# A one-core decoder layer on Trainium2: the running sum of w_down is kept in the output tensor in DRAM instead of in SBUF for ten of eleven groups

## The reference

```python
x = _layernorm(DN_ALPHA * x + mix @ w_out[l], ln1_g[l], ln1_b[l])
gate, up = jnp.split(x @ w_gate_up[l], 2, axis=-1)
x = _layernorm(DN_ALPHA * x + (jax.nn.silu(gate) * up) @ w_down[l], ln2_g[l], ln2_b[l])
```

## Time and profile before

| | |
|---|---|
| median of 3 runs | 2036.58 us (2036.22 to 2038.27) |
| profiled execution, its own time | 2035.88 us |
| profiled execution, span | 2034.1 us |
| PE busy | 2016.6 us, 99% |
| DVE busy | 1310.5 us, 64% |
| ACT busy | 677.4 us, 33% |
| POOL busy | 361.4 us, 18% |
| DMA traffic | 214.06 MB, mean 105 GB/s |
| granted TensorE clock, mean | 0.997 |

### The profile page before, as it was taken

The page is one execution under the profiler, slowest core; times in us unless marked ns, Lnnn a source line. Parts: engine busy times, 40 slices in busy tenths (PEclk is TensorE's granted clock), DMA queues, the critical chain, the costliest instruction groups (busy, mean ns, idle before and its releaser), DMA issues.

```text
span 2034.1 us, 32431 instructions
## 1 busy us (share of the span) xinstructions
PE 2016.6 (99%) x12539; PEld 1785.3 (88%) x12539; DVE 1310.5 (64%) x1876; ACT 677.4 (33%) x1080; POOL 361.4 (18%) x175
## 2 busy tenths in 40 slices
PE   9999999899999999999999999999999999999999
PEld 7777888666888998999989999898999989999897
DVE  3079994463114885766857677585766857677577
ACT  3011000364000543442524334243442524334253
POOL 2555556144566400000000000000000000000000
PEclk9999999899999999999999999999999999999999
DMA  7333434400524324242424424233242424424242
GB/s 216 94 83 83 103 97 110 130 22 29 217 86 125 83 83 125 84 135 74 120 89 116 124 82 126 84 94 125 83 135 74 120 88 117 123 82 126 83 144 96
DMA packets 292234, 214.06 MB, mean 105 GB/s; under 512 B 9574, under 2 KB 256166, under 8 KB 290314
## 3 DMA queue, kind: packets, MB, share of 16 engines
q1 hardware_dynamic: 292026, 211.97, 35.3%
q10 hardware_dynamic: 80, 0.13, 0.0%
HBM read 207.76 MB, written 4.19 MB: 104 GB/s over the span
## 4 chain that ended last, share of the span: by engine, by line
PE 96%; DMA 1%; DVE 1%; ACT 0%; SPq 0%; issue 0%; DVEq 0%
PE psum L1104 14%; PE psum L1102 13%; PE psum L1106 13%; PE psum L1143 8%; PE psum L1144 8%; PE psum L1145 8%; PE psum L752 6%; PE psum L754 6%; PE psum L753 6%; PE psum L986 3%; PE psum L988 3%; PE psum L987 3%; PE psum L965 1%; PE psum L902 1%; PE psum L893 1%; PE psum L953 1%
## 5 line engine op out<-in xcount | busy, mean ns | idle before, releaser
L1102 PE MATMUL psum<-act,w_room 128*128 128x256 f32 x1344 | 374.7, 279 | 0.0
L1104 PE MATMUL psum<-act,w_room 128*128 128x256 f32 x1344 | 374.7, 279 | 0.0
L1106 PE MATMUL psum<-act,w_room 128*128 128x256 f32 x1344 | 374.7, 279 | 0.0
L1906 DVE TENSOR_TENSOR w_room<-raw,w_room 128x1024 fp32r<-128x1024 f32 x210 | 256.8, 1223 | 127.2 <-ACT w_room L1406 126.9
L1906 DVE TENSOR_TENSOR w_room<-raw_c,w_room 128x1024 fp32r<-128x1024 f32 x164 | 201.0, 1225 | 176.3 <-ACT w_room L1406 176.3
L1406 ACT CAST w_room<-raw 128x1024 fp32r<-128x1024 f32 x212 | 223.3, 1053 | 227.2 <-PE psum L1145 132.8
L1143 PE MATMUL psum<-w_room,h 128*128 128x512 f32 x672 | 261.7, 389 | 0.0
L1144 PE MATMUL psum<-w_room,h 128*128 128x512 f32 x672 | 261.6, 389 | 0.0
L1145 PE MATMUL psum<-w_room,h 128*128 128x512 f32 x672 | 261.4, 389 | 0.0
L1104 PEld LDWEIGHTS psum<-act,w_room 128*128 128x128 f32 x1344 | 252.7, 188 | 0.4
L1102 PEld LDWEIGHTS psum<-act,w_room 128*128 128x128 f32 x1344 | 252.7, 188 | 0.4
(11 more groups left out here) (272 smaller groups left out, 3480.2 us busy)
## 6 DMA issues: line engine op xcount, KB each, us to landing
raw_c<-in_w_gate_up SPq DMA_DIRECT2D x84, 512.0 KB, 4.1
raw<-in_w_gate_up SPq DMA_DIRECT2D x84, 512.0 KB, 5.0
raw_c<-in_w_down SPq DMA_DIRECT2D x82, 512.0 KB, 3.8
raw<-in_w_in SPq DMA_DIRECT2D x30, 1024.0 KB, 5.6
raw<-in_w_out SPq DMA_DIRECT2D x16, 1024.0 KB, 5.1
acc<-in_x SPq DMA_DIRECT2D x1, 4096.0 KB, 12.4
raw<-in_w_gate_up SPq DMA_DIRECT2D x4, 1024.0 KB, 5.7
proj<-in_x_t SPq DMA_DIRECT2D x3, 1024.0 KB, 8.9
```

The lines of the kernel that those rows point to most:

```text
L1102: nc.tensor.matmul(out_ap, stat_hi[:, cols], mov_hi[:, k, :], start=opens and k == 0, stop=False, skip_group_check=not opens)
L1104: nc.tensor.matmul(out_ap, stat_hi[:, cols], mov_lo[:, k, :], start=False, stop=False, skip_group_check=not opens)
L1106: mm = nc.tensor.matmul(out_ap, stat_lo[:, cols], mov_hi[:, k, :], start=False, stop=k == kh - 1, skip_group_check=not opens)
L1906: nc.vector.tensor_tensor(lo, src, hi.bitcast(F32), ALU.subtract).then_inc(lo_ready, 1)
```

## The change

In the ten groups of the loop, DVE no longer adds. The scaled x is first stored to `out` (SP, once, 4 MB). In each group ACT copies the 16 finished banks into `acc`, which is now a place for copies, not for the sum, and POOL issues for each of them a DMA of 256 KB that adds the region of `acc` to the same region of `out` in DRAM. ACT may begin the copies of a group when all 16 DMAs of the group before have landed (`down_summed`, handed on as `slots_free`). After the loop SP waits for all 160 DMAs and loads the 4 MB from `out` back into `acc`; this wait and this load stand in SP's queue ahead of the loads of the last group. The eleventh group adds into `acc` as before.

```diff
@@ SP
             load_b12(3 * P, 1)
+            sp.wait_ge(scaled, TT)
+            nc.sync.dma_start(out_dram, acc[:, :, :]).then_inc(base_stored, 16)
             with sp.Fori(0, FF_GROUPS - 1) as g:
...
             tail_q = c43.q + 7
+            sp.wait_ge(down_summed, 16 * 16 * last)
+            nc.sync.dma_start(acc[:, :, :], out_dram).then_inc(acc_loaded, 16)
             released(c42, 3)
@@ POOL
+            pool.wait_ge(base_stored, 16)
+            for g in range(FF_GROUPS - 1):
+                if g > 0:
+                    pool.wait_ge(down_summed, 16 * 16 * g)
+                nc.gpsimd.sem_inc(slots_free, 1)
+                for n in range(4):
+                    for i in range(TT):
+                        pool.wait_ge(tile_added, g * 16 + (TILES0 + 16 + 4 * n + i + 1))
+                        cols = slice(n * SEQ, (n + 1) * SEQ)
+                        nc.gpsimd.dma_start(out_dram[:, i, cols], acc[:, i, cols], accum_op=ALU.add)\
+                            .then_inc(down_summed, 16)
@@ ACT
+            def keep_down(g, n, i):
+                if i < TT - 1:
+                    act.wait_ge(down_tile, g * 12 + (3 * n + i + 1))
+                else:
+                    act.wait_ge(gran_done, g * PER_GROUP + (DOWN_AT + 2 * n + 2))
+                nc.scalar.copy(acc[:, i, n * SEQ:(n + 1) * SEQ], psum[:, i, :]).then_inc(tile_added, 1)
+
             def down(g, held, following):
+                act.wait_ge(slots_free, g + 1)
                 for d in range(8):
-                    act.wait_ge(gran_done, g * PER_GROUP + (DOWN_AT + d + 1))
+                    if d % 2 == 0:
+                        act.wait_ge(gran_done, g * PER_GROUP + (DOWN_AT + d + 1))
+                    else:
+                        for i in range(TT):
+                            keep_down(g, d // 2, i)
@@ DVE
-            def add_down(g, n, i):
-                cols = acc[:, i, n * SEQ:(n + 1) * SEQ]
...
-                nc.vector.tensor_tensor(cols, cols, psum[:, i, :], ALU.add).then_inc(tile_added, 1)
-
...
             def down(g, held, following):
-                ve.wait_ge(scaled, TT)
                 for d in range(8):
-                    if d % 2 == 1:
-                        for i in range(TT):
-                            add_down(g, d // 2, i)
...
             late_piece(1)
+            ve.wait_ge(acc_loaded, 16)
```

More of the change, by code:

```diff
@@ L394, in build @@
         stored = sem("stored")
+        base_stored = sem("base_stored")
+        down_summed = sem("down_summed")
+        slots_free = sem("slots_free")
+        acc_loaded = sem("acc_loaded")
         win = w_in[0].rearrange("(k p) n -> p k n", p=P)
@@ L1819, in add_out @@
                 link(nc.vector.bn_stats(stats[:, i, n, :], cols))
-            def add_down(g, n, i):
-                cols = acc[:, i, n * SEQ:(n + 1) * SEQ]
-                if i < TT - 1:
-                    ve.wait_ge(down_tile, g * 12 + (3 * n + i + 1))
-                else:
-                    ve.wait_ge(gran_done, g * PER_GROUP + (DOWN_AT + 2 * n + 2))
-                nc.vector.tensor_tensor(cols, cols, psum[:, i, :], ALU.add).then_inc(tile_added, 1)
             def add_tail(i, n, bank, tiles, count, with_stats):
```

## The result

The kernel after takes 2058.45 us (median of 4 runs, 2055.59 to 2062.21), beside 2036.4 us (2034.16 to 2038.27) for the kernel before on the same chip: ratio 1.0113, 95% interval 1.0101 to 1.0126. It is 22 us slower. The prediction of no change, 2036.6 us with a range to 2050, was wrong.

What follows compares the result with a forecast made beforehand. The prediction took PE, busy all 122 us of each period, to bound the kernel; its six terms were each 0 on PE's path, so it forecast 2036.6 us, range 2034 to 2050.

Steps and rivals of the forecast that it cites:

- What bounds the kernel now: Step on the ten-group loop: PE is busy all 122.00 us of each period and waits for nothing.
- DVE's adds go: Term for DVE's 160 dropped adds, 104.1 us in all beside PE's work: gain on the path 0.
- ACT's copies come: Term for ACT's 160 bank copies of 586 ns, 9.4 us a period, earlier than the adds were: cost 0.
- Roundings move behind the last copy: Term for ACT's roundings starting 0.6 us after the end of a piece, needed 16 us on: cost 0.
- The 4 MB store: Term for storing scaled x to `out` before the loop: at most 15.6 us, done before the next load, cost 0.
- 160 adding DMAs: Term for POOL's sums into `out` in the loop: 2.3 us each, not even a queue, cost 0.
- c: Time of each adding DMA when they follow each other: taken as 2.3 us, bounds 0.78 and 6.0.
- The wait and the 4 MB load at the end: Term for SP's queue after the loop: cost 0 if the last sum lands by 1944, 3.7 us each.
- rival (a): Slower at the end only, sums landing after 1944: +21 us at 5 us each, +37 at 6.0; chance 0.09.
- (b): Slower in every group, sums over 7.7 us each and ACT stopping at `slots_free`: +270 us at 9 us; chance 0.04.
- (c): Weight loads crowded by the sums in the loop, DMA share 0.6 or so: +80 us; chance 0.04.
- (d): Faster, PE stepping quicker in the loop because DVE leaves PSUM alone: 4.8 us in all; chance 0.03.

Runs made afterwards that it cites:

- e2: The kernel after without the 160 adding DMAs, ACT's copies and the 4 MB store and load kept: 2034.78 us.
- e6: The kernel after with PE's loop written out, so without a backward branch: 2034.04 us, ratio to the kernel before 0.9993.
- e9: The kernel after with POOL issuing a group's 16 adding DMAs only when the stage's last bank has been copied: 2065.45 us.
- e10: The kernel before, DVE still adding, plus 160 adding DMAs of 256 KB from DRAM to DRAM issued by POOL: 2059.79 us.
- e7: The kernel before, DVE still adding, plus 16 plain DRAM-to-DRAM copies of 256 KB per group issued by POOL: 2036.26 us.
- e11: The kernel after with plain stores from `acc` to `out` in place of the adding DMAs, same queue and waits: 2036.18 us.
- e12: The kernel before with PE's loop over the middle nine groups written out: 2035.36 us, ratio to the kernel before 1.0004.
- e8: The kernel after with PE's loop cut between the first and second piece of w_down, ahead of the first sum: 2036.53 us, ratio 1.0012.
- e5: The kernel before with PE's loop cut between the second and third chunk of a group: 2049.36 us.
- e18: The kernel before with PE's loop cut between the second and third chunk and 136 semaphore increments ahead of PE's first work: 2081.58 us.
- e13: The kernel after with 64 semaphore increments ahead of PE's first work, shifting its code in memory: 2067.62 us.
- e14: The kernel after with 128 semaphore increments ahead of PE's first work, shifting its code in memory: 2076.49 us.
- e15: The kernel after with 192 semaphore increments ahead of PE's first work, shifting its code in memory: 2083.21 us.

## Why the prediction was wrong

**What bounds the kernel now** held, and held the flaw. PE was the bound and waited for nothing in the loop, so the only question was what would make it wait. I asked this of the semaphores, and of the data that crosses the DMA engines: weights, sums, the 4 MB. PE's own instructions cross them too, nine packets of 16 KB in a period. The page of the kernel before lists them as a queue; I passed over it because 0.4% of the engines' time is no load. It is not the load that counts but the moment: at the loop's backward branch PE lives on what is queued. Before, the fetch at the branch was covered, since no period has a gap; by at most about half a microsecond, by the estimate from its packets above.

**DVE's adds go**: gain 0, as forecast; 73 to 75 us of DVE in a period. **ACT's copies come**: right in size and place. The copies take 587 ns at the median, the first of the stage above starts at 906.96, 0.24 us behind the rounding that began at 905.67, and e2 and e6 show no cost. **Roundings move behind the last copy**: 0, by the same two runs.

**The 4 MB store** landed 14.7 us after its issue (e2's page), within the bound of 15.6, and SP's next loads were not late.

**160 adding DMAs** is the step that failed, twice. The term itself was mis-sized: c was taken as 2.3 us and is 3.2 (e9), within its bounds of 0.78 and 6.0 and below both thresholds, 3.7 and 7.7. The sums of a stage were in flight almost without a break, not "not even a queue", and a 256 KB sum landed after 6.1 us, not under 4. And "cost: 0 in the loop" left their other effect out: for about 55 of 122 us (907.9 to 962.9) they are in flight, the branch lies in these 55, and PE's instructions came late there eight times. This second omission is what cost the time; at its measured size the term alone would still have left the sum at 0. The estimate by the Trainium skill's page Collectives: The Full Stack, section "The bandwidth ceiling" (half the rate of a copy, 1.6 us), was further off. As to the engines' time, its rule is about right where both operands are in DRAM, 1.8 times (e10 and e7), and short where the source is in SBUF, 2.6 times (the kernel after and e11).

**The wait and the 4 MB load at the end** cost nothing, as forecast, but by less than was thought: the last copy ended at 1947.5, the load of the sum could be issued at 1966.14, so the last sum landed about 18.6 us behind it, where 23 us were allowed and some 10 expected. In e6, where the loop runs at full pace, the load is issued at 1941.1, 3 us ahead of the limit; counted from the stage's first issue (1884.9) that is 3.5 us for each sum, beside a threshold of 3.7. With c taken as 2.3 that this term stayed at 0 was luck. e9 crossed the limit by 28.1 us and paid 27.3: the mechanism of rival (a) and its limit of 1944 were right, the kernel only stayed on its good side. Its argument that latency isn't paid 16 times in a queue held in part: it was paid about once for every two or three.

**The rivals.** (b) didn't happen: the profile shows no wait of ACT on `slots_free`. (c) is the nearest. It had the DMA share go to 0.6 (it is 0.60) and the weight loads late, for 80 us. They were hardly slower, 4.4 us instead of 3.8 for a piece of w_down, and the profile puts no wait of PE down to them; the crowding hit another reader. (d) had no gain behind it: e6 and e12 have loops of the same length, and their intervals overlap. The chance of slower, 0.18, was too low for an edit that takes the DMA share of a kernel without slack on PE from 0.35 to 0.60, with every user of those engines but one looked at.

**Still open**: the depth of PE's queue, why e8's loop is not fetched again, and what holds a packet of instructions up behind adding DMAs (the queues of the DMA engines, or the memory behind them); no run parts these. A version faster than the kernel before was not found.

## What to carry to other kernels

Where an engine has no slack, list all that it takes through the DMA engines, its instruction packets included, and look up where its loops branch back. Before traffic is put beside such a branch, move the branch or write the loop out; a wait that ends in "issue", or in a releaser that was long done, at the same place in every iteration, points to the fetch of code. And keep idle gaps of the matmul engine short: those of up to 1.7 us cost little more than themselves, those of 2.1 us or more cost the clock as well, another 1.7 us.

## What the runs showed of the hardware

- A backward branch of PE's loop can cost 1.9 us with the DMA engines idle (e5: stretch 15.1 us over 8 branches), 3.8 us with the same code elsewhere in memory (e18: 30.4), and nothing behind 512-column matmuls (before) or without a fetch (e8).
- PE goes on 1.35 to 1.88 us after the packet of instructions that it lacked has ended (84 waits in eleven runs).
- An adding DMA of 256 KB takes 3.2 us in a queue of its kind (e9, where POOL has at most three of them issued at a time) and 6.1 us from issue to landing; the plain store of the same tile lands in 2.7 us (e11).
- Instruction packets are 16 KB each; the loop written out takes seven in a period of 122 us, as a loop nine, except in e8.
- A semaphore increment on PE takes about 0.15 us (e13, e14, e15).
